# Two attention stages of a diffusion transformer step: fillers behind fixed token blocks instead of spread evenly, and a projection between the last transposes

## What is computed

```python
def diff_attention(q, k, v, lam):
    s = jnp.einsum('bqjhd,bkjhd->bjhqk', qb, k) * scale      # 4 heads, j = 0, 1
    pr = jax.nn.softmax(s, axis=-1)
    pr = pr[:, 0] - lam * pr[:, 1]
    return jnp.einsum('bhqk,bkhe->bqhe', pr, v)
...
def mla_attention(q_nope, q_rope, k_nope, k_rope, v):        # 8 heads
    s = (q_nope . k_nope + q_rope . k_rope) * scale
    return jnp.einsum('bhqk,bkhe->bqhe', jax.nn.softmax(s), v)
...
br = jnp.stack([y_hy, y_da, y_mla], axis=2) * silu(paths)
y_br = jnp.einsum('blni,nid->blnd', br, p['w_branch'][l])
merged = jnp.sum(sigmoid(merge) * y_br, axis=2)
```

## Time and profile before

| | us |
|---|---|
| median of 3 runs (2076.57 to 2081.05) | 2078.33 |
| the profiled execution | 2078.16 |
| its span in the profile | 2076.1 |
| TensorE busy | 1917.4 |
| VectorE busy | 1129.1 |
| ScalarE busy | 639.1 |
| GpSimd busy | 549.5 |
| mean granted TensorE clock | 0.974 |

### The profile page before, as it was taken

The page is one execution under the profiler, slowest core; times in us unless marked ns, Lnnn a source line. Parts: engine busy times, 40 slices in busy tenths (PEclk is TensorE's granted clock), DMA queues, the critical chain, the costliest instruction groups (busy, mean ns, idle before and its releaser), DMA issues.

```text
span 2076.1 us, 28060 instructions
## 1 busy us (share of the span) xinstructions
PE 1917.4 (92%) x11444; PEld 1639.1 (79%) x11444; DVE 1129.1 (54%) x1551; ACT 639.1 (31%) x1132; POOL 549.5 (26%) x248
## 2 busy tenths in 40 slices
PE   6799989999999999998968999899999999999995
PEld 4568679887786777898966787898788777779985
DVE  3548678355343443477676886844453434444734
ACT  2221321244332444321233222123342344442121
POOL 0211114222222111267221121331222301115641
PEclk9899999999999999999989999999999999999998
DMA  9001112111120110353620010221113100114431
GB/s 338 31 27 35 41 51 72 52 57 46 52 108 21 34 31 31 107 190 121 233 92 31 31 51 21 72 68 55 41 52 107 41 29 21 41 47 159 136 102 51
DMA packets 50158, 151.83 MB, mean 73 GB/s; under 512 B 11050, under 2 KB 12586, under 8 KB 48752
## 3 DMA queue, kind: packets, MB, share of 16 engines
q1 hardware_dynamic: 46432, 135.89, 19.5%
q10 hardware_dynamic: 3600, 14.16, 2.0%
HBM read 143.43 MB, written 6.59 MB: 72 GB/s over the span
## 4 chain that ended last, share of the span: by engine, by line
PE 74%; DVE 14%; ACT 5%; issue 3%; POOL 2%; SPq 1%; DMA 1%; ACTq 0%; DVEq 0%; POOLq 0%
PE PS L757 17%; PE PS L762 16%; PE PS L758 16%; PE PS L793 5%; PE PS L926 3%; PE PS L1044 2%; PE PS L781 2%; PE PS L828 2%; PE PS L831 2%; PE PS L977 2%; PE PS L810 1%; ACT work L1097 1%; ACT Wh L1097 1%; DVE MG L1565 1%; DVE work L1774 1%
## 5 line engine op out<-in xcount | busy, mean ns | idle before, releaser
L1725 POOL TENSOR_TENSOR Wl<-W,Wh 128x1024 fp32r<-128x1024 f32 x196 | 455.8, 2327 | 1344.1 <-ACT Wh L1097 1300.5
L757 PE MATMUL PS<-Hh,Wh 128*128 128x320 f32 x2112 | 636.6, 316 | 19.6 <-ACT Wh L1097 8.5
L758 PE MATMUL PS<-Hl,Wh 128*128 128x320 f32 x2112 | 626.5, 311 | 0.0
L757 PEld LDWEIGHTS PS<-Hh,Wh 128*128 128x128 f32 x2112 | 400.7, 190 | 48.2 <-issue 27.8
L758 PEld LDWEIGHTS PS<-Hl,Wh 128*128 128x128 f32 x2112 | 400.7, 190 | 1.4 <-issue 1.2
L762 PE MATMUL PS<-Hh,Wl 128*128 128x320 f32 x2112 | 331.4, 309 | 0.9 <-POOL Wl L1725 0.9
L762 PEld LDWEIGHTS PS<-Hh,Wl 128*128 128x128 f32 x2112 | 315.1, 188 | 1.4 <-POOL Wl L1725 1.4
L1097 ACT ACTIVATE work<-PS 128x640 f32<-128x640 f32 (+10 forms) x322 | 180.5, 574 | 353.6 <-PE PS L793 97.8
L1360 DVE TENSOR_REDUCE st<-PS 128x1 f32<-128x640 f32 (+1 forms) x160 | 114.9, 718 | 282.8 <-PE PS L810 176.3
L1097 ACT ACTIVATE Wh<-W 128x1024 fp32r<-128x1024 f32 x196 | 185.2, 950 | 35.3 <-PE PS L762 18.1
L1208 ACT ACTIVATE th<-PS 128x640 f32<-128x640 f32 x64 | 45.0, 704 | 360.1 <-PE PS L762 360.1
(11 more groups left out here) (187 smaller groups left out, 2489.9 us busy)
## 6 DMA issues: line engine op xcount, KB each, us to landing
W<-in_w_in SPq DMA_DIRECT2D x132, 512.0 KB, 3.5
W<-in_w_branch SPq DMA_DIRECT2D x48, 256.0 KB, 2.6
work<-in_w_mod_rows ACTq DMA_DIRECT2D x23, 512.0 KB, 3.8
pmod_w<-in_w_mod SPq DMA_DIRECT2D x8, 1024.0 KB, 17.1
W<-in_w_out SPq DMA_DIRECT2D x16, 512.0 KB, 4.4
late_modulation_w<-in_w_mod_rows SPq DMA_DIRECT2D x9, 512.0 KB, 6.1
work<-in_x_sample SPq DMA_DIRECT2D x2, 2048.0 KB
x_mid<-work SPq DMA_DIRECT2D x1, 2560.0 KB, 8.5
```

The source lines that it names most:

```text
L757: pe.matmul(out, Wh[:, b, kk, :], xh[:, kk, t], start=kk == 0, stop=False)
L758: pe.matmul(out, Wh[:, b, kk, :], xl[:, kk, t], start=False, stop=False)
L1725: return pool.tensor_tensor(out, in_, high.bitcast(f32), ALU.subtract)
```

## The change

`attention_steps` gets two more arguments: the blocks of a head behind whose scores a filler stands, one each, and what stands behind each of the last two transposes. In the differential attention these are blocks 0 to 3, in the latent one blocks 0 and 2, so that there `mgate` stands at block 0 and `mbranch` at block 2; in the differential attention `mgate` stands at blocks 0 and 2, `mbranch` at 1 and 3. `dqkv 0` stands between the last two transposes of the differential attention, the spreads `dab` behind `dqkv 3` and `mms 0` instead of ahead of them. VectorE makes lambda at step `v 0` instead of the first scores, and the last unit's weights one step earlier.

```diff
-def attention_steps(tag, heads, fillers, before=None, behind=None):
+def attention_steps(tag, heads, fillers, behind_units, tail, before=None, behind=None):
...
-        upto = len(fillers) * (u + 1) // len(units)
-        steps += fillers[taken:upto]
-        taken = upto
+        if t in behind_units:
+            steps += fillers[taken:taken + 1]
+            taken += 1
         if u >= LAG:
             steps.append((tag + "_ptrans", u - LAG))
-    return steps + [(tag + "_ptrans", len(units) - LAG + n) for n in range(LAG)] + [(tag + "_pv", heads - 1)]
+    for n in range(LAG):
+        steps += [(tag + "_ptrans", len(units) - LAG + n)] + tail[n]
+    assert taken == len(fillers)
+    return steps + [(tag + "_pv", heads - 1)]
...
-    s += attention_steps("da", DAH, merge_steps(0), behind=lambda h: [("dasq", h), ("dams", h)])
-    s += [("dasq", 3), ("dqkv", 0), ("dams", 3), ("dqkv", 1), ("dart", 0), ("dqkv", 2)] + [("dab", h) for h in range(DAH)]
-    s += [("dqkv", 3), ("mms", 0), ("dqkv", 4), ("kr", 0), ("mms", 1)]
+    s += attention_steps("da", DAH, merge_steps(0), range(4), ([("dqkv", 0)], []), behind=lambda h: [("dasq", h), ("dams", h)])
+    s += [("dasq", 3), ("dqkv", 1), ("dams", 3), ("dqkv", 2), ("dart", 0)]
+    s += [("dqkv", 3), ("mms", 0)] + [("dab", h) for h in range(DAH)] + [("dqkv", 4), ("kr", 0), ("mms", 1)]
...
-    s += [step for t in range(NT) for step in head(0, t)] + attention_steps("ml", MH, merge_steps(1), head)
+    s += [step for t in range(NT) for step in head(0, t)] + attention_steps("ml", MH, merge_steps(1), (0, 2), ([], []), head)
...
-                    elif kind == "da_score":
+                    elif kind == "v" and i == 0:
                         if i == 0:
                             dve.wait_ge(*after("lam_exp", l, 1))
                             link(TT(lamc[:, 2:3], lamc[:, 4:5], lamc[:, 5:6], ALU.subtract))
                             link(TS(lamc[:, 6:7], lamc[:, 2:3], lamc[:, 0:1], -1.0, ALU.add, ALU.mult))
                             link(TT(lamc[:, 7:8], subln[:], lamc[:, 1:2], ALU.mult))
+                    elif kind == "da_score":
...
-                    elif kind == "da_ptrans" and i == DAH * NT - 1:
-                        da_weights(l, i)
+                    elif kind == "da_ptrans" and i == DAH * NT - 2:
+                        da_weights(l, i + 1)
```

## The result

The changed kernel takes 2115.12 us (median of 4 runs, 2113.28 to 2116.01), the kernel before 2078.74 in runs on the same chip: ratio 1.0172, 95% interval 1.016 to 1.0184. The forecast was slower, 2096 us, at most 2106. It is slower by 36.4 us, twice as much as forecast.

What follows compares the result with a forecast made beforehand. TensorE, busy 1917.4 of 2076.1 us, was taken to bound the kernel; -5.3 + 9.4 + 9.4 - 5.1 + 5 + 5 = +18.4 on 2078.2 gave about 2096 us, range 2083 to 2106.

Steps and rivals of the forecast that it cites:

- What bounds the kernel: Whole kernel: TensorE is busy 1917.4 of 2076.1 us, so a moved step is worth only the time TensorE stands still.
- The differential attention: Differential stage: new waits of 6.9 us for removed ones of 9.4 (9.7 in layer 1), minus 5.3 for both layers.
- The weights of `dqkv 3`: End of differential attention: the weight lands late behind four transfers; TensorE waits 4.25 and 5.15 us, 9.4 in both layers.
- The latent attention: Latent stage: stops of 19.2 us for 14.5, plus 4.7 a layer, 9.4 in both.
- the chain: Latent stage: VectorE's work ahead of block 2's weights makes TensorE wait 2.15 us in heads 2, 4, 6; 3.4 in head 0.
- The clock: Lower granted clock behind waits: minus 5.1 for removed waits, plus 5 behind weight waits, plus 5 behind other new ones.
- three of ten, plus 5: Three of ten new waits in both layers followed by the lower clock: plus 5 us, ends 0 and 17.
- plus 5 behind the weight waits: Both waits for the weight of `dqkv 3` followed by the lower clock: plus 5 us.
- the ten stops: Expected new waits in both layers: latent heads 0, 2, 4, 6 and the last differential value product.
- the 5.1 removed: Lower clock behind three of today's waits in the attention stages goes with them: minus 5.1 us.
- The terms without the clock: Sum of the differential, weight and latent terms: -5.3, +9.4 and +9.4, together 13.5 us.
- The clock falls at every wait: Rival for the new waits: the lower clock follows each, 12 us more, 2108 us; chance 0.10.

Runs made afterwards that it cites:

- Weight first: The changed kernel with SP issuing the weight of `dqkv 3` ahead of its wait for the last sum of squares and of the four transfers: 2098.88 us.
- half-filled: The changed kernel with two overwritten 512-column matmuls before block 2's transposes in latent heads 0, 2, 4, 6 and 7: 2098.72 us.
- query part later: The changed kernel with VectorE's preparation of the next head's rotated query at block 4 instead of block 3: 2097.67 us.

## Why the prediction was right and wrong

**What bounds the kernel: right.** Every microsecond is in the four attention stages, as waits of TensorE or as its clock.

**The differential attention: right in mechanism, its gain too high.** 0.77 + 0.58 = 1.35 for two heads (forecast 1.4), 1.80 at the value product (1.8, with the high part ahead on ScalarE), 1.06 at the spreads (0.85). Without the weight waits the idle time of the two stages fell by 1.7 and 2.0, 3.7 where I had 5.3. The placement alone on the kernel before, with the old tail, has 3.7 less idle time too, and no gain in time, since the clock took it.

**The weights of `dqkv 3`: right in mechanism, a quarter too dear.** Waits of 3.52 and 3.69 instead of 4.25 and 5.15, 7.2 for 9.4: the landings took 7.4 and 7.7 instead of the 8.0 and 8.7 that I had taken from the earlier trace rows. Weight first takes both waits away.

**The latent attention: right.** Stops of 1.94 (2.15 forecast), 1.07 + 2.01 in head 0 (3.4), 0.47 before the next head's scores (0.6). I had 4.7 a layer for the chain. The half-filled kernel has no lower clock in this stage and takes 211.0 for the 208.0 of before, which had 1.7 us of clock in it: 3.0 + 1.7 = 4.7. It may be up to 0.8 less, since the filling of head 7 (1.88) is longer than the stop there (1.08). In head 0 POOL meets the addition, as foreseen. The orders of time on POOL and VectorE:

```profile
687.82 2.36 POOL L1729 TENSOR_TENSOR Wl<-W,Wh 128x1024 fp32r<-128x1024 f32 x1 [3.21 <-ACT Wh L1100]
```

```profile
688.61 2.25 DVE L1568 TENSOR_TENSOR MG<-MG,th 128x640 f32<-128x640 f32 x1
```

It ends at 690.86, 0.68 after the subtraction.

**The clock: the step that failed.** I wrote "three of ten, plus 5", and plus 5 behind the weight waits. The weight waits were right: 3.4 + 1.7 = 5.1. Of the ten stops the eight latent ones were all followed (17.0), the two of 1.80 before the value product not. And two kinds that I had not counted among the ten were: the spreads' 1.06 (5.1 in both layers) and the 1.74 before `mv 0` (3.4), which the kernel before passes at full clock. That is 30.6 less the 5.1 removed, 25.5, where I had 4.9. TensorE's busy time grew by 18.2. The terms without the clock came out at -3.7 + 7.2 + 9.4 = 12.9, where I had 13.5, so that nearly all of the miss is this one term.

I took a frequency (three of eight) from a kernel whose stops stand elsewhere and used it as a chance per stop; behind the stops of this placement it was 8 of 8. (Three of eight would also have been nearly four of ten, not three.) The rival *The clock falls at every wait* had 2108 and 0.10, and even this was too low, because it left out the stops near 1 us. The range's upper end, 2106, should have reached it: the term's own ends were 0 and 17. The Trainium skill (TensorE: Matmul & The Clock Gate, A second HAM failure mode: psum-queue depth-cycling) says that frequent short stops between groups of matmuls can make the clock swing between its levels; these runs agree, and show a price (16.4 us for eight stops). I had read it and not given it a chance of its own.

**Settled and open.** Shown: the weight wait (weight first), the chain of VectorE and the pair in it (query part later), the clock's share (half-filled). Not shown: a rule for which stop is followed, and what makes two executions of one kernel differ in it.

## What to carry to other kernels

Removing waits from a TensorE-bound kernel is worth what its clock lets it be: read the granted clock of short stretches behind every stop, and price a new stop of about 2 us among transposes and scores at up to twice its length. Compare several executions before you explain a difference of 2 to 5 us, and see which of them the profile is of. Before moving a step, list what each in-order queue issues with it: here one weight behind four transfers of 2.3 MB cost 12 us, and the line that cures it gave 16. Where stops can't be removed, filling part of them with matmuls of no use can pay, if the filling is shorter than the stop.

## What the hardware showed that I had not expected

The same instructions with the same stop of 1.94 us were followed by the lower level (1.2 of 2.4 GHz) in one kernel and not in another, and repeated their pattern when the changed kernel was run once more. Stops of 1.04 to 1.06 before the spreads were followed in both layers of every kernel that has them, stops of 1.08 before the transposes of heads 2, 4 and 6 in none of six; one of 1.08 with two shorter ones right behind it was followed in both layers. Useless matmuls of 1.88 us in stops of 1.94 made the program 16.4 us faster.

An addition in SBUF that begins under a POOL subtraction ended 0.67 to 0.68 us after it in each case shown (1.40, 1.51, 2.25 and 2.27 us long, 0.82 when free), while the product just ahead of it, which reads PSUM, took its usual 0.82 under the same subtraction. The Trainium skill (SBUF — State Buffer, SBUF: two separate sides) says that VectorE operations with two inputs in SBUF and GpSimd lock each other out of a shared port for a whole instruction. The traces agree; that the addition needs only 0.68 behind the subtraction, less than its 0.82, stays unexplained.
